# A layered transformer kernel on one core: the eight relative-bias products are moved from a row of their own to places inside and between two projections

## The reference, cut to what matters

```python
h = rmsnorm(x, g_pre)
proj = h @ w_in                                   # 1024 -> 6144 columns
q_a, k_a, v_a, g_a = proj[..., 0:4096]            # attention, 8 heads of 128, and its gate
x_m, z_m = proj[..., 4096:5120], proj[..., 5120:]
...
s_own = einsum(qf, k_own) + bias_h[:, t5_bucket(dist)]    # the relative bias, 8 heads
...
x_c = silu(causal_depthwise_conv(x_m, conv_w, conv_b))
q_m, k_m = blockdiag_proj(x_c, wq_m), blockdiag_proj(x_c, wk_m)
v_m = blockdiag_proj(x_m, wv_m)
...
y_m = (h_m + skip * x_c) * silu(z_m)
```

## Time and profile before

| | |
|---|---|
| three timed runs | 2177.08 us median (2176.83 to 2180.48) |
| the profiled execution, whole | 2178.38 us |
| its span, first to last instruction | 2176.5 us |
| PE busy | 2097.7 us, 96% of the span |
| VectorE busy | 1566.4 us, 72% |
| ScalarE busy | 1251.6 us, 58% |
| mean granted clock of TensorE | 0.983 of full speed |

### The profile page before, as it was taken

How to read it: one execution, slowest core, us unless ns; L and a number is a source line. 1 busy time by engine, 2 the same in 40 slices (tenths; PEclk the granted TensorE clock), 3 DMA queues, 4 the chain that set the end, 5 groups by cost and what they waited for, 6 DMA issues and landing times.

```text
span 2176.5 us, 30224 instructions
## 1 busy us (share of the span) xinstructions
PE 2097.7 (96%) x10504; PEld 1710.9 (79%) x10504; DVE 1566.4 (72%) x2095; ACT 1251.6 (58%) x1624; POOL 16.9 (1%) x31
## 2 busy tenths in 40 slices
PE   7999998889999999999998999999999999999998
PEld 5787758749998768998656888888888888888887
DVE  6256535686664765554357989999898989989897
ACT  2311236544444364443246877788787878878786
POOL 0000000000000000001000000000000000000000
PEclk9999999999999999999999999999999999999999
DMA  8567644235563315654315999999899999989995
GB/s 308 168 246 259 225 172 165 84 114 190 166 203 98 115 59 195 192 179 122 116 59 194 367 338 365 362 331 384 320 377 332 364 353 344 384 319 381 329 363 212
DMA packets 272062, 536.14 MB, mean 246 GB/s; under 512 B 29156, under 2 KB 80877, under 8 KB 271725
## 3 DMA queue, kind: packets, MB, share of 16 engines
q1 hardware_dynamic: 266061, 527.54, 67.9%
q10 hardware_dynamic: 5072, 4.36, 0.7%
q0 software_dynamic: 848, 3.15, 0.4%
HBM read 531.87 MB, written 3.14 MB: 246 GB/s over the span
## 4 chain that ended last, share of the span: by engine, by line
PE 89%; DVE 6%; ACT 2%; issue 1%; SPq 1%; DMA 0%; ACTq 0%; DVEq 0%
PE sum L1523 12%; PE bank L1505 9%; PE bank L1507 9%; PE bank L1506 9%; PE bank L719 9%; PE sum L1164 6%; PE sum L781 5%; PE bank L1181 3%; PE bank L1183 3%; PE bank L1182 3%; PE bank L1457 2%; PE bank L735 1%; PE sum L1271 1%; PE bank L1491 1%; PE sum L1537 1%
## 5 line engine op out<-in xcount | busy, mean ns | idle before, releaser
L2914 DVE TENSOR_TENSOR x_lo<-ring,x_hi 128x1024 fp32r<-128x1024 f32 x672 | 784.6, 1220 | 73.6 <-ACT x_hi L2065 48.7
L2065 ACT ACTIVATE x_hi<-ring 128x1024 fp32r<-128x1024 f32 x648 | 672.9, 1060 | 152.0 <-PE bank L1507 87.6
L1505 PE MATMUL bank<-x_hi,hg_hi 128*128 128x512 f32 x896 | 354.7, 396 | 1.5 <-DVE x_lo L2914 1.5
L1507 PE MATMUL bank<-x_hi,hg_lo 128*128 128x512 f32 x896 | 349.8, 390 | 0.0
L1506 PE MATMUL bank<-x_lo,hg_hi 128*128 128x512 f32 x896 | 349.1, 390 | 0.0
L2273 DVE TENSOR_TENSOR w_lo<-ring,w_hi 128x1024 fp32r<-128x1024 f32 x130 | 157.9, 1224 | 116.1 <-ACT w_hi L1875 114.4
L719 PE MATMUL bank<-hT,ring 128*128 128x256 f32 x1024 | 232.0, 388 | 2.3 <-DVE hT L2160 2.3
L719 PEld LDWEIGHTS bank<-hT,ring 128*128 128x128 f32 x1024 | 198.8, 195 | 35.0 <-issue 7.0
L1875 ACT ACTIVATE w_hi<-ring 128x1024 fp32r<-128x1024 f32 x130 | 136.9, 1060 | 147.6 <-PE bank L1183 76.3
L1507 PEld LDWEIGHTS bank<-x_hi,hg_lo 128*128 128x128 f32 x896 | 168.3, 188 | 35.9
L1505 PEld LDWEIGHTS bank<-x_hi,hg_hi 128*128 128x128 f32 x896 | 168.6, 188 | 35.1 <-DVE x_lo L2914 1.9
(11 more groups left out here) (481 smaller groups left out, 2852.7 us busy)
## 6 DMA issues: line engine op xcount, KB each, us to landing
ring<-in_sw_we_gate SPq DMA_DIRECT2D x114, 1024.0 KB, 7.1
ring<-in_sw_we_up SPq DMA_DIRECT2D x112, 1024.0 KB, 7.1
ring<-in_sw_we_down SPq DMA_DIRECT2D x112, 1024.0 KB, 7.0
ring<-in_w_in SPq DMA_DIRECT2D x36, 1024.0 KB, 7.4
ring<-in_w_ff SPq DMA_DIRECT2D x32, 1024.0 KB, 5.4
ring<-in_ada_w SPq DMA_DIRECT2D x24, 1024.0 KB, 7.1
ring<-in_w_out SPq DMA_DIRECT2D x12, 1024.0 KB, 7.5
ring<-in_cv_w_gate SPq DMA_DIRECT2D x11, 1024.0 KB, 5.2
```

The lines of the kernel that those rows point to most:

```text
L1505: mm(ps[b][:, :], hg_hi[:, k, :], hi[:, cols], start=(k == 0), stop=False)
L1507: last = mm(ps[b][:, :], hg_lo[:, k, :], hi[:, cols], start=False, stop=(k == KC - 1))
L2065: go(f(x_hi[:, hp % MSLOTS, :], ring[:, s, lo:lo + PIECE // 2], ACT.Copy), c.sig("hi_ready", hp))
L2914: v.tensor_tensor(x_lo[:, hp % MSLOTS, :], ring[:, s, lo:lo + PIECE // 2], x_hi[:, hp % MSLOTS, :].bitcast(F32), ALU.subtract).then_inc(c. ...
```

## The change

The eight bias products no longer stand in a row. A new parameter of proj_T, mid, is called between the two halves of a projection job. A new function cols_rel projects 512 columns in two jobs and puts four bias products around them: one inside the first job, one between the jobs, one inside the second, one behind. The projection of 4608 takes heads 0 to 3, the one of 5120 heads 4 to 7. The two waits ahead of the bias products move ahead of the projection of 4608. ScalarE's copies follow the new order, and its eight Silu over the convolution are split in two groups of four between them; the DMA to relrow is issued behind the copy of head 7, now behind both copies of the projection of 5120. The pieces of a projection are freed by its second job, ahead of the fourth bias product.

```diff
-            def proj_T(stage, w, c0, q, hT=hT, fresh=None):
+            def proj_T(stage, w, c0, q, hT=hT, fresh=None, mid=lambda: None):
 
                 b = J.fill(pe, stage, q)
                 for j in range(2):
+                    if j:
+                        mid()
                     for k in range(KC):
...
+            def rel(h):
+                b = J.fill(pe, "rel", h)
+                done(mm(ps[b][:, 0:511], relw[0:33, h, :], C("rel")[0:33, :], start=True, stop=True), "rel", h)
+
+            def cols_rel(col, h):
+
+                w, keys = chunks("w_in", col)
+                for q in range(2):
+                    s = proj_T("b1p", w, q * 256, col // 256 + q, mid=lambda: rel(h + 2 * q))
+                    if q < 1:
+                        rel(h + 1)
+                free(keys, s)
+                rel(h + 3)
+
             cols_T("b1p", "w_in", 4096)
-            cols_T("b1p", "w_in", 4608)
+            pe.wait_ge(*c.at("rel_wide"))
+            pe.wait_ge(c.sem("consts_in"), 16)
+            cols_rel(4608, 0)
             for g in range(1, 4):
                 columns_of(g)
             ada_columns(0)
-            pe.wait_ge(*c.at("rel_wide"))
-            pe.wait_ge(c.sem("consts_in"), 16)
-            for h in range(HEADS1):
-                b = J.fill(pe, "rel", h)
-                done(mm(ps[b][:, 0:511], relw[0:33, h, :], C("rel")[0:33, :], start=True, stop=True), "rel", h)
-            cols_T("b1p", "w_in", 5120)
+            cols_rel(5120, 4)
             ada_columns(1)
...
-            for q in range(16, 20):
+            def rel(h):
+                copy(relrep[:, h, 0:511], ("rel", h), 511)
+
+            def conv_silu(*ks):
+
+                for k in ks:
+                    act.wait_ge(*c.at("conv", k))
+                    do(f(xcT[:, k, :], xcT[:, k, :], ACT.Silu), c.sig("conv_ready", k))
+
+            for q in range(16, 18):
                 copy(pair(xmT, q - 16), ("b1p", q))
+            rel(0)
+            copy(pair(xmT, 2), ("b1p", 18))
+            rel(1)
+            rel(2)
+            copy(pair(xmT, 3), ("b1p", 19))
+            rel(3)
             for g in range(1, 4):
                 columns_of(g)
-            for h in range(HEADS1):
-                copy(relrep[:, h, 0:511], ("rel", h), 511)
+            conv_silu(0, 1, 2, 3)
+            rel(4)
+            copy(pair(mix1, 4), ("b1p", 20), func=ACT.Silu)
+            rel(5)
+            conv_silu(4, 5, 6, 7)
+            rel(6)
+            copy(pair(mix1, 5), ("b1p", 21), func=ACT.Silu)
+            rel(7)
             act.dma_start(relrow, relrep[:, :, 0:511]).then_inc(c.sem("relrow_out"), 16)
-            for k in range(KC):
-                act.wait_ge(*c.at("conv", k))
-                do(f(xcT[:, k, :], xcT[:, k, :], ACT.Silu), c.sig("conv_ready", k))
-            for q in (20, 21):
-                copy(pair(mix1, q - 20 + 4), ("b1p", q), func=ACT.Silu)
             act.wait_ge(c.sem("relrow_out"), 16)
```

## The result

The changed kernel takes 2190.3 us (median of 6 runs, 2185.96 to 2194.28) against 2176.95 before (median of 6, 2170.99 to 2183.67): ratio 1.0062, 95% interval 1.0045 to 1.008. That is 13.4 us slower, where 10.5 were forecast. The profiled execution took 2186.80 us with a span of 2185.0.

A forecast was written before the change was run, and what follows sets the result against it. TensorE (PE) was taken as the bound, with 89% of the chain. Shift 8.3 plus clock 2.2 gave +10.5 us: 2188.9 from the profiled 2178.38, 2187.6 as median; range 2179.1 to 2192.7.

The forecast's parts named there:

- (1): PE up to the block-diagonal products: they start at 66.9 us instead of 74.49, 7.6 us early.
- (2): relrow DMA: issued at 67.0 us instead of 58.26; its landing holds PE, shifting the fifth block-diagonal product by +8.3 us.
- d: Time from relrow's issue to its landing: taken as 18.5 us; the shift of PE's products is d - 10.2.
- turn-taking end: relrow's duration if its queue and the weight pieces' queue take turns on the engines: 20.0 us.
- low end: Shortest duration for relrow, from issue to landing: 9.0 us.
- (3): Clock after PE's standstill at the block-diagonal products: half clock loses 2.2 us, bounds 0 and 2.6.
- (4): First fall of the clock, within 48 to 49 us before: taken as avoided; if it stays, at most 2.2 us.
- A: Rival: relrow quicker, d between 9 and 14, gain and loss cancel, 2175.9 to 2183.1 us; chance 0.15.
- B: Rival: not slower, relrow moves at the pieces' rate, about 6.4 us, 2173.3 us without a fall; chance 0.07.
- C: Rival: the first clock fall stays, up to 2.2 us more, +12.7, 2189.8 us; chance 0.15.

The follow-up runs named there:

- Experiment 1: Kernel before, with only the relrow DMA issued later, behind ScalarE's two Silu copies of the projection of 5120: 2191.58 us against 2174.4, ratio 1.0087.
- Experiment 3: Changed kernel, with SyncE's sixteenth weight piece and all behind it held until relrow has landed: 2184.08 us against 2174.4 before, ratio 1.0041.
- experiment 6: Changed kernel, all eight bias products in pairs at the projection of 4608, relrow issued behind the last copy: 2174.53 us against 2174.4 before, ratio 0.9997.
- experiment 9: Changed kernel with pairs, the last inside 5120's first job, 383-value bias rows, relrow wait behind four block-diagonal copies: 2169.44 us against 2178.04 before, ratio 0.9962.
- experiment 8: Kernel before, bias products in their row, 383 of 511 values, relrow wait behind the first four block-diagonal copies: 2173.27 us against 2177.0, ratio 0.9981.
- experiment 4: Changed kernel, with ScalarE's relrow wait moved from ahead of the first block-diagonal copy to ahead of the fifth: 2185.21 us against 2177.0 before, ratio 1.0041.
- experiment 2: Changed kernel, with the relrow transfer cut to head 0, one eighth of the bytes: 2174.83 us against 2174.4 before, ratio 0.9999.

## Why the prediction was right, and where its sizes were off

The sign, the mechanism and the place are as forecast: the DMA is issued later, PE reaches its block-diagonal products earlier, and the wait between them takes the place of the row's half clock. Experiment 1 shows it without any product moved. The measured +13.4 us lies in the stated range. By steps:

**(1) PE 7.6 us early: measured 2.9 in the profile.** Two things. The first 80 records took 19.52 us, where 17.4 is the price at full clock (15 to 43 us in the earlier trace rows divides to 0.2177 each). The same stretch before (first) and after (second), the columns as in the earlier trace rows:

```profile
16.00:18.00 2.00, 2.00 (x11) 1.75 (x10) 1.29 (x3) 0.54 (x2) 0.00 (x0) 1.00 1.13 241
...
16.00:18.00 2.00, 2.00 (x6) 1.58 (x5) 1.16 (x2) 0.70 (x2) 0.00 (x0) 1.00 1.16 252
```

Six records in 2 us are what PE does at a granted clock of 0.50 (before, 58 to 60 us: x6), eleven what it does at 1.00. So PE worked at the lower level until about 20 us, ahead of anything that the change touches, though the column reads 1.00. It is the execution's luck, and in either order: the same 80 records took 17.50 in the profiles of experiments 3, 6 and 9 and 19.00 to 19.61 in five others; the 128 of the old order took 27.86 before, but 29.65 and 29.89 in experiments 1 and 8. The rest is a mis-sized term. I priced a bias product at 0.90 us, its price in the row. Placed singly, it takes 1.05 (34.96 to 36.01), and the half job behind it 3.65 (36.01 to 39.66) instead of 3.48: 4.70 for both where 4.38 was counted. Two of the eight stand ahead of small products and not of a half job, so this is 8 x 0.15 + 6 x 0.17 = 2.2 us. The last 0.4 of the miss of 4.7 lies in the start (15.50 for 15.35) and in the small products and the half job behind them. A pair takes 1.90 and the half job again 3.65 (experiment 6), so the extra is paid per insertion, not per product. What makes an insertion dearer no run here shows.

**(2) relrow issued at 67.0: measured 71.48,** by the same 2.1 of the start and 2.4 of the rest. **d of 18.5: measured 20.84**; 21.0 and 20.4 in experiments 1 and 4, so it repeats. The value lay close to the turn-taking end of 20.0; I had shaded it down towards the old 17.5, and that shading was the error. Experiment 3 tells what the bounds should have been. The low end of 9.0 was 1.1 us to the first packets plus 7.9 of all sixteen engines. Alone, relrow took 9.2 us of sixteen engines (61.3% of 15 us), spread over 10.3 by its tail, and 2.8 more from the last packet to the landing, which the bound left out: 14.2.

**(3) Clock behind the standstill, 2.2: measured 2.5.** The eight products from 93.09 take 9.62 where eight at full clock take 7.15 (experiment 4, at 71.67); the clock is back within 98 to 99.

**(4) First fall avoided: so it was**, in the changed kernel's profile and in the four others of the experiments with single products. With pairs up to the transposes it came in two profiles of three, behind the last pair.

Summed by the profile: (1) and (2) shift the fifth block-diagonal product by 93.09 - 78.0 = 15.1 (forecast 8.3), (3) makes it 17.6 at the vm products. Without the 2.1 of the start it is 15.5, against 10.5 forecast: 2.4 by the price of insertions and what goes with it, 2.3 by d, 0.3 by the clock. The medians say 13.4. The 2 us between are open: the forecast passed the shift on whole to the end, while in this pair of profiles falls of the clock at other places took 17.6 down to 8.5, and the profiles are too few to tell which of them belong to the order of PE's list and which to the execution. That the median came out nearer to the forecast than the opening did is nothing that the forecast foresaw.

**The rivals.** A (gain and loss cancel, d of 9 to 14) fell with d. Its time came true only where the transfer was made smaller (experiment 2) or sent early (experiment 6, with a d of 23.2); alone, with a d of 14.2, the kernel was still 0.41% slower. B (relrow at the pieces' rate, 6.4 us) is refuted harder than I thought: not even 0.26 MB landed that fast. The fit of the Trainium skill's page "DMA: Bandwidth & Descriptors" (section "Anatomy of one DMA") is given there for DMAs that GpSimd issues by its software path, while relrow goes out on ScalarE's hardware queue (q10); the prediction didn't say so. The estimate from it, 6.8 us, is less than half of what relrow takes with nothing beside it, 14.2; the measurement decides. C didn't come.

## What to carry to other kernels

Before work is moved on the engine that bounds a kernel, follow what the moved results feed: here a 2 MB transfer was issued 13 us later and its landing stood one wait ahead of the next copies. A wait that shows 1.3 us of idle time today can be the next bound in full; its slack is what counts, not its length. And moving light products between long ones paid only with the transfer behind them made smaller, sent early and waited for later: all of it together gave 0.4%, of which the narrower rows and the later wait gave 0.2% with the products left in their row; moving the products alone lost 0.6%.

## What the runs showed of the hardware that I had not expected

- Writing 2.09 MB to DRAM in 1024 rows of 2044 bytes took 14.2 us alone, and 17.5, 20.4, 20.8, 21.0 and 23.2 us beside loads of weights, though it starts near the rate of those loads (382 to 398 GB/s against 413). Of the 14.2, 2.8 lie behind its last packet.
- A product of 33 rows by 511 columns costs 0.86 us in a row of its like at full clock (the copies behind the first three start at 46.22, 47.08 and 47.93) and 1.05 between projections, where it also lengthens the half job behind it by 0.17.
- One execution differs from the next by where the clock falls: stretches of 3.4 us or several of them, each 3.4 costing 1.7 where PE is busy. Of 26 runs of the kernel before in one session, the fastest took 2169.57 us at a mean clock of 0.989, the slowest 2182.51 at 0.982.
- In the first 5 us of the projections the granted clock reads 1.00, but their first 80 records took from 17.50 to 19.61 us in the profiles of the changed order. The number of records in a stretch tells the clock there, the column doesn't.
